# RWKV-7 mixer: the chunk recurrence as one transfer product and one addition a step

## The chip, the core and the metric

The kernel runs on one core of one Trainium2 chip. The metric is the device time of one execution in microseconds. The text uses the profiler's names: PE is TensorE (matmuls), PEld its weight loads, DVE VectorE, ACT ScalarE, POOL GpSimd, SP the queue that issues the transfers. One matmul call on float32 data stands in the trace as two matmul records and two weight-load records; one on float32r data as one of each.

## The reference, cut to what matters

Two decoder layers over 512 positions of width 1024. Each layer is a half feed-forward, a mixer and a half feed-forward. The even layer's mixer is called "ab": an input projection (22 blocks of 128 columns), a Griffin branch, and RWKV-7 time mixing with 8 heads of width 64. This last part is what the change is about:

```python
def step(state, inp):
    r_t, w_t, k_t, v_t, kk_t, a_t = inp
    sa = jnp.einsum('bhvk,bhk->bhv', state, kk_t)
    state = (state * w_t[:, :, None, :]
             - sa[..., None] * (kk_t * a_t)[:, :, None, :]
             + v_t[..., None] * k_t[:, :, None, :])
    return state, jnp.einsum('bhvk,bhk->bhv', state, r_t)
_, y = lax.scan(step, state0, xs)
```

Behind it come a group norm for each head, a bonus term, a gate and the output projection (8 blocks, "ab_out"). The odd layer has another mixer ("c", gated DeltaNet), which the change leaves alone.

## The kernel before

It is one program with an instruction stream for each engine, ordered by hand and joined by semaphores; `wait_ge` makes an engine wait, `then_inc` counts up. Weights stream from HBM through four slots (`RAW`), and ACT and DVE split each into a high and a low float32r part (`WS`), so that each product of the dense blocks is three matmuls (lines 590 to 592). `pe.Fori(1, 4)` is a loop of three passes whose body stands once in PE's stream; a Python `for` writes its body out as many times as it runs.

The 512 positions are cut into 8 chunks (`c`) of 64. A 128-partition tile holds two heads, so there are four blocks `b` of two heads. They are worked in two pairs, `q` = 0 and 1, and in a pair `z` is 0 or 1, so `b = 2q + z`. Every small product is a 64x64 matmul. It reads one half of the partitions (`r`) and writes one half: the same, or for chunks 4 to 7 often the other one (`crossed(r)`). A list in the order `four_ways` goes round all four quarters of the array, `chunk_blocks` and `heads_of` only round the two on the diagonal.

For each pair PE makes the in-chunk products (`triangle_product`, `key_products`, `back_product`), and then inverts a triangular matrix for each head and chunk by doubling. A level is `pe_level_u`, a mask on DVE (line 1989), `pe_level_xx`, a copy on ACT (line 1332), and a transposition on DVE (lines 1979 and 1981). Levels 1 to 3 of both `z` are the `Fori` loop of lines 894 to 902, which also turns one block of keys (`tokens_turned`, `KT` for pair 0, `BT` for pair 1) in each pass. `inside` makes the part of the solution that needs no state: `GT` (the right side for the solve) and `YI` (its outputs). The result of the inversion is `XTF`.

Then comes the recurrence over the chunks (lines 925 to 957), with all 8 heads at once in each product. A step needs, one behind the other: the prediction from the state (L937), an addition on DVE (L2241), the solve with `XTF` (L948), a copy on ACT (L1523), the product with the keys `BT` (L955), and the subtraction on DVE that gives the next state (L2254). The products `KT` with `VT` (L942) and the outputs of the chunk before (`outputs`, L918 and L921) fill gaps. Behind the last chunk DVE adds the outputs (`YF`, L2260), and PE makes the sums for the group norm (L962, L966), the gate (L968) and the output projection.

Of the kernel before, what the change touches and what calls it, by code (L numbers as in the profile page):

```python
# [11 lines left out]
P = 128  # L12
SEQ = 512
# [134 lines left out]
def hybrid_trunk_kernel(nc, x, params, const, w_gate, w_up, w_down, ab_in, ab_out, lru_a, lru_x,  # L148
# [28 lines left out]
    with ExitStack() as ctx:  # L177
# [111 lines left out]
        GT, YI = quad("GT", H_AT + 2 * Q), quad("YI", H_AT + 3 * Q)  # L289
# [24 lines left out]
        SDEC = at("SDEC", SPARE_AT + SEQ + 96, [P, 4, CHUNK])  # L314
# [20 lines left out]
        def ab_mix(t):  # L335
# [22 lines left out]
        predict_mm, predict_added, solve_mm, solve_read, state_mm, state_ready = (sem("predict_mm"), sem("predict_added"), sem("solve_mm"), sem("solve_read"),  # L358
                                                    sem("state_mm"), sem("state_ready"))
# [69 lines left out]
        def head_block(first, rows, e, upper=False):  # L429
# [20 lines left out]
            (predict_mm, 7), (predict_added, 7), (solve_mm, 8), (solve_read, 8), (state_mm, 14), (state_ready, 7),  # L450
# [3 lines left out]
            (exp_ready, 3), (fold_ready, 4), (kk_sq, 4), (ss_max, 4), (bon_in, 4), (bon_mm, 4), (bv_ready, 4), (staged, 6), (level_begun, 34), (fm_ready, 4),  # L454
# [122 lines left out]
        def _(pe):  # L577
# [83 lines left out]
            def tokens_turned(first, src, b, upper, across):  # L661
# [4 lines left out]
                tr.then_inc(tr_mm, 1)  # L666

            def pe_first_u(q, z):
# [4 lines left out]
                if z:  # L673
                    pe.wait_ge(tr_read, 4 * q + 5)
                elif q:
                    pe.wait_ge(xx_read[z], 5)
                else:
                    pe.wait_ge(z_read, AB_BLOCKS)
# [63 lines left out]
            for phase in plan:  # L742
# [19 lines left out]
                if phase == "ab":  # L762
# [85 lines left out]
                    def back_product(q, z):  # L848
# [19 lines left out]

                    for q in range(2):
# [3 lines left out]
                        if q == 0:  # L873
# [3 lines left out]
                            tokens_turned(4, KF, 0, upper=False, across=True)  # L877
                            pe_first_u(q, 0)
                        else:
# [4 lines left out]
                            tokens_turned(4, AL, 0, upper=False, across=False)  # L884
# [9 lines left out]
                        with pe.Fori(1, 4) as l:  # L894
                            pe_level_u(q, 1, l)
                            pe_level_xx(q, 0, l)
                            pe.wait_ge(tr_read, l + 4 * q + 4)
                            pe.wait_ge(staged, l + 3 * q)
                            pe.sem_inc(level_begun, 1)
                            tokens_turned(2, STAGE, 0, upper=False, across=q == 0)  # L900
                            pe_level_u(q, 0, l + 1)
# [9 lines left out]
                    heads_of = [(b, slice(h * CHUNK, (h + 1) * CHUNK)) for b in range(4) for h in range(2)]  # L911

                    def outputs(c, blocks):

                        cc = slice(c * CHUNK, (c + 1) * CHUNK)
                        for b in blocks:
                            for r in (slice(0, CHUNK), slice(CHUNK, P)):
                                mm = pe.matmul(BANK[4 + b][r, cc], GT[r, b, cc], MBT[r, b, cc], start=True, stop=c == 0)  # L918
                            if c:
                                for r in (slice(0, CHUNK), slice(CHUNK, P)):  # L920
                                    mm = pe.matmul(BANK[4 + b][r, cc], SH[r, c, b, :], RF[r, b, cc], start=False, stop=True)  # L921
                            if c == NCHUNK - 1:
                                mm.then_inc(out_mm, 1)

                    for c in range(NCHUNK):
                        cc = slice(c * CHUNK, (c + 1) * CHUNK)
                        if c == 0:
                            for z in range(2):
                                pe.wait_ge(xx_read[z], 10)
                                pe.wait_ge(token_read[z], 4)  # L930
                                pe.wait_ge(mat_ready[z], 8)
                            pe.wait_ge(tr_read, 12)
                            pe.wait_ge(fold_ready, 4)
                        else:
                            pe.wait_ge(state_ready, c)
                            for b, r in heads_of:
                                mm = pe.matmul(BANK[0][r, b * CHUNK:(b + 1) * CHUNK], CPRE[r, b, cc], SH[r, c, b, :], start=True, stop=True)  # L937
# [1660 lines left out]
```

## Time and profile before

| what | us |
|---|---|
| median of 3 runs (2129.04 to 2129.66) | 2129.57 |
| the profiled execution, its own time | 2129.91 |
| span of its trace | 2128.1 |
| of it: inversion of both pairs, 519.4 to 581.2 | 61.8 |
| recurrence over the chunks, 581.2 to 609.6 | 28.4 |
| group norm, gate and first products of the output projection, 609.6 to 636.5 | 26.9 |
| DVE starts the first `YF` | 609.57 |

The profiled execution is 0.34 us above the median. The places in the second part of the table are microseconds from the start of the span. Nearly all of the rest of the span is dense matmuls that follow one another with no gap, so the time of the kernel is the dense products plus what PE loses in the mixers' cores.

### The profile page before, as it was taken

The numbers are of one execution on the slowest core, as the hardware profiler recorded it, in microseconds if no ns is written. First come the engines' busy times: TensorE is split into PE (matmuls) and PEld (weight loads), VectorE is DVE, ScalarE is ACT, GpSimd is POOL, SyncE is SP. The second block draws the span as 40 slices with busy tenths as digits, with TensorE's granted clock in tenths as the row PEclk, the third lists the DMA queues.
The fourth block names the chain that finished last, engine by engine and source line by source line (L and its number), as shares of the span: only waits on it lengthen the run. The fifth ranks groups of instructions, "written<-read, shape, count | busy, mean of one in ns | idle before, by whom it ended". The sixth has DMA issues, their size and how long they took to land. (4 is left out here: it accounts for less than half of the span.)

```text
span 2128.1 us, 33196 instructions
## 1 busy us (share of the span) xinstructions
PE 2077.8 (98%) x13332; PEld 1705.0 (80%) x13332; DVE 1124.0 (53%) x1451; ACT 778.0 (37%) x1175; POOL 165.7 (8%) x120
## 2 busy tenths in 40 slices
PE   7999999999799999999999999999999999999998
PEld 6888888777777888888888888877888878888886
DVE  5444444568757444443444443478776675444422
ACT  4332223383434223322322332245665443323221
POOL 2000011002302000011000001101110120000010
PEclk9999999999999999999999999999999999999999
DMA  4222322320012222332222232221111122222321
GB/s 176 93 99 99 111 95 80 104 70 21 23 61 88 100 96 92 113 100 93 80 99 98 91 118 96 80 81 51 51 51 47 56 80 89 99 99 95 113 95 53
DMA packets 48265, 182.65 MB, mean 86 GB/s; under 512 B 6320, under 2 KB 6576, under 8 KB 48048
## 3 DMA queue, kind: packets, MB, share of 16 engines
q1 hardware_dynamic: 48176, 181.39, 24.8%
q8 instruction: 65, 1.06, 0.2%
q14 instruction: 24, 0.20, 0.0%
HBM read 179.27 MB, written 2.10 MB: 85 GB/s over the span
## 5 line engine op out<-in xcount | busy, mean ns | idle before, releaser
L590 PE MATMUL banks<-H,WS 128*128 128x512 f32 x1840 | 730.8, 397 | 11.4 <-DVE H L1997 8.0
L592 PE MATMUL banks<-H,WS 128*128 128x512 f32 x1840 | 717.6, 390 | 0.0
L591 PE MATMUL banks<-H,WS 128*128 128x512 f32 x1840 | 717.5, 390 | 0.0
L1279 ACT ACTIVATE WS<-RAW 128x1024 fp32r<-128x1024 f32 (+1 forms) x308 | 347.1, 1127 | 931.5 <-PE banks L592 928.1
L1913 DVE TENSOR_TENSOR WS<-RAW,WS 128x1024 fp32r<-128x1024 f32 (+1 forms) x308 | 404.4, 1313 | 231.4 <-ACT WS L1279 231.2
L590 PEld LDWEIGHTS banks<-H,WS 128*128 128x128 f32 x1840 | 346.1, 188 | 91.0 <-DVE WS L1913 11.9
L592 PEld LDWEIGHTS banks<-H,WS 128*128 128x128 f32 x1840 | 346.0, 188 | 72.8
L591 PEld LDWEIGHTS banks<-H,WS 128*128 128x128 f32 x1840 | 346.3, 188 | 71.4 <-issue 2.4
L590 PE MATMUL banks<-A,WS 128*128 128x512 f32 x704 | 273.9, 389 | 0.0
L591 PE MATMUL banks<-A,WS 128*128 128x512 f32 x704 | 273.9, 389 | 0.0
L592 PE MATMUL banks<-A,WS 128*128 128x512 f32 x704 | 273.9, 389 | 0.0
L1780 POOL TENSOR_TENSOR ACC<-ACC,US 128x512 f32<-128x512 f32 x49 | 92.8, 1894 | 1364.2 <-issue 1006.3
L1953 DVE TENSOR_TENSOR US<-banks,RSTD 128x512 f32<-128x512 f32 x88 | 60.8, 691 | 248.8 <-PE banks L592 248.8
L1953 DVE TENSOR_TENSOR GS<-banks,RSTD 128x512 f32<-128x512 f32 x88 | 60.8, 691 | 180.1 <-PE banks L592 180.1
L590 PEld LDWEIGHTS banks<-A,WS 128*128 128x128 f32 x704 | 132.1, 188 | 27.7
L592 PEld LDWEIGHTS banks<-A,WS 128*128 128x128 f32 x704 | 132.1, 188 | 27.3
L591 PEld LDWEIGHTS banks<-A,WS 128*128 128x128 f32 x704 | 132.1, 188 | 27.3
L1925 DVE SCALAR_TENSOR_TENSOR X<-banks,X 128x512 f32 (+1 forms) x48 | 33.1, 690 | 158.8 <-PE banks L592 158.8
L1316 ACT ACTIVATE A<-US 128x512 f32 (+1 forms) x88 | 55.7, 633 | 47.5 <-DVE US L1960 47.2
L1960 DVE TENSOR_TENSOR US<-GS,US 128x512 f32<-128x512 f32 x88 | 60.9, 693 | 9.1
L1965 DVE TENSOR_TENSOR A<-US,A 128x512 f32 (+1 forms) x88 | 60.3, 685 | 2.8 <-ACT A L1316 2.8
L1311 ACT ACTIVATE GS<-GS 128x512 f32<-128x512 f32 x88 | 54.1, 615 | 13.6 <-DVE GS L1953 13.6
(388 smaller groups left out, 1660.5 us busy)
## 6 DMA issues: line engine op xcount, KB each, us to landing
RAW<-in_w_gate SPq DMA_DIRECT2D x88, 512.0 KB, 3.2
RAW<-in_w_up SPq DMA_DIRECT2D x88, 512.0 KB, 3.2
RAW<-in_w_down SPq DMA_DIRECT2D x64, 704.0 KB, 4.0
RAW<-in_c_in SPq DMA_DIRECT2D x32, 512.0 KB, 3.2
RAW<-in_ab_in SPq DMA_DIRECT2D x22, 512.0 KB, 3.2
RAW<-in_ab_out SPq DMA_DIRECT2D x8, 512.0 KB, 5.6
RAW<-in_c_out SPq DMA_DIRECT2D x8, 512.0 KB, 3.2
X<-in_x SPq DMA_DIRECT2D x4, 512.0 KB, 7.1
```

What stands on the lines that cost most here:

```text
L590: pe.matmul(bank[:, :], high[:, cols], upper, start=first and j == 0, stop=False)
L591: pe.matmul(bank[:, :], high[:, cols], lower, start=False, stop=False)
L592: mm = pe.matmul(bank[:, :], low[:, cols], upper, start=False, stop=last and j == len(rows) - 1)
L1279: act.activation(WS[:, 0, c % SPLIT, 0:cols] if dst is None else dst, RAW[:, c % RING, 0:cols], ACT.Copy).then_inc(hi_ready, 1)
L1311: act.activation(GS[:, j, :], GS[:, j, :], ACT.Silu).then_inc(silu_ready[j], 1)
L1316: act.activation(A[:, 0, 2 * i + j, :], US[:, j, :], ACT.Copy).then_inc(ahi_ready[j], 1)
L1780: pool.tensor_tensor(ACC[:, :], ACC[:, :], US[:, j, :], ALU.add).then_inc(acc_ready[j], 1)
L1913: vec.tensor_tensor(WS[:, 1, c % SPLIT, 0:cols], RAW[:, c % RING, 0:cols], WS[:, 0, c % SPLIT, 0:cols].bitcast(F32), ALU.subtract).then_in ...
L1925: vec.scalar_tensor_tensor(X[:, 2 * i + j, :], bank[:, :], factor, X[:, 2 * i + j, :], ALU.mult, ALU.add).then_inc(x_ready[j], 1)
L1953: vec.tensor_tensor((GS, US)[k][:, j, :], (GATE, UP)[k][j][:, :], RSTD[:, :], ALU.mult).then_inc((gs_ready, us_ready)[k][j], 1)
L1960: vec.tensor_tensor(US[:, j, :], GS[:, j, :], US[:, j, :], ALU.mult).then_inc(prod_ready[j], 1)
L1965: vec.tensor_tensor(A[:, 1, 2 * i + j, :], US[:, j, :], A[:, 0, 2 * i + j, :].bitcast(F32), ALU.subtract).then_inc(act_ready[j], 1)
```

## The change

The step of the recurrence is linear in the state, so a whole chunk can be written as one 64x64 matrix for each head (the transfer, `MT`) and one addition (`NS`): state(c+1) = MT(c)' state(c) + NS(c). Both are made ahead of the recurrence, for all chunks of a block.

- The prediction keys `CPRE`, weighted by the decay of the chunk before (`prior_fold` on POOL, into `PRIOR_STAGE`), are turned on PE into `PT`, one block in pair 0's prologue and one in each pass of its loop, and copied by ACT (`prior_copied`).
- `inner(b)` applies `XTF` to `GT` and to `PT` at once: 32 matmul calls a block, one behind the other on the same quarter. ACT (for blocks 2 and 3 half of it DVE) copies both with the sign turned: the new `GT`, and `WT`.
- `transfer(b)` (12 calls) gives `MT` = `WT` with `BT` plus a diagonal of decays (`DIAG`, made on POOL; added on POOL for blocks 0 and 1, on DVE for 2 and 3). `additions(b)` (28 calls) gives `NS` = `KT` with `VT` plus `BT` with `GT`.
- `corrections(b)` (14 calls) and an addition on DVE fold the in-chunk correction into the queries `RF`. `within(b)` (16 calls) makes the outputs that need no state, and `carried(c)` (8 calls) adds those from the state.
- A step is then `state_step(c)` (8 calls) and `state_added(c)` on DVE, for c = 1 to 6. The old loop over the chunks goes.
- Pair 1's loop of levels is written out, with `inner`, `transfer` and `additions` of blocks 0 and 1 between its levels. Pair 0's loop stays a loop, its body longer by one `tokens_turned`.
- `back_product` and the turning of `AL` go round four quarters where they went round two. `YI`, `MT`, `DIAG`, `PT` and `NS` take places of tiles that are done with. Ahead of the levels PE also waits for the `inside` copies of the second block (`token_read[1]`).

```diff
-GT, YI = quad("GT", H_AT + 2 * Q), quad("YI", H_AT + 3 * Q)
+GW = at("GW", H_AT + 2 * Q, [P, 2, 4, SEQ])
+GT, WT = GW[:, 0], GW[:, 1]
+NS, MT = quad("NS", H_AT), quad("MT", ACT_AT + 4 * Q)
+YI, DIAG = quad("YI", ACT_AT + 8 * Q), quad("DIAG", ACT_AT + 9 * Q)
+PT, PRIOR_STAGE = quad("PT", WS_AT), at("PRIOR_STAGE", WS_AT + Q, [P, 1, SEQ])
...
                 pe.wait_ge(mat_ready[z], 4 * q + 3)
-                for r, c in chunk_blocks():
+                for r, a, c in four_ways:
                     cc = slice(c * CHUNK, (c + 1) * CHUNK)
-                    mm = pe.matmul(BANK[4 * z + 2][r, cc], AL[r, b, cc], RF[r, b, cc], start=True, stop=True)
+                    mm = pe.matmul(head_block(4 * z + 2, a, c), AL[r, b, cc], RF[r, b, cc], start=True, stop=True)
                 mm.then_inc(mat_mm[z], 1)
...
+            def inner(b):
+                q, z = divmod(b, 2)
+                pe.wait_ge(xx_read[z], 5 * q + 5)
+                pe.wait_ge(token_read[z], 2 * q + 2)
+                if b == 0:
+                    pe.wait_ge(prior_read, 4)
+                    pe.wait_ge(token_read[1], 4)
+                if b == 1:
+                    pe.wait_ge(m_copied, 1)
+                for r, a, c in four_ways:
+                    cc = slice(c * CHUNK, (c + 1) * CHUNK)
+                    pe.matmul(head_block((6, 6, 0, 4)[b], a, c), XTF[r, b, cc], GT[r, b, cc], start=True, stop=True)
+                    mm = pe.matmul(head_block((6, 6, 0, 4)[b], a, c, upper=True), XTF[r, b, cc], PT[r, b, cc], start=True, stop=True)
+                mm.then_inc(inner_mm, 1)
...
+            def transfer(b):
+                inner_done(b)
+                pe.wait_ge(tr_read, 9 + b)
+                if b >= 2:
+                    pe.wait_ge(n_read, b - 1)
+                for r, a, c in four_ways:
+                    if 0 < c < NCHUNK - 1:
+                        cc = slice(c * CHUNK, (c + 1) * CHUNK)
+                        mm = pe.matmul(head_block((6, 6, 6, 2)[b], r, c), WT[a, b, cc], BT[a, b, cc], start=True, stop=True)
+                mm.then_inc(m_mm, 1)
+            def additions(b):
+                inner_done(b)
+                if b == 0:
+                    pe.wait_ge(m_copied, 2)
+                if b == 1:
+                    pe.wait_ge(tr_read, 12)
+                for r, a, c in four_ways:
+                    if c < NCHUNK - 1:
+                        cc = slice(c * CHUNK, (c + 1) * CHUNK)
+                        to = head_block((6, 2, 0, 4)[b], r, c)
+                        pe.matmul(to, KT[a, b, cc], VT[a, b, cc], start=True, stop=False)
+                        mm = pe.matmul(to, BT[a, b, cc], GT[a, b, cc], start=False, stop=True)
+                mm.then_inc(n_mm, 1)
+            def corrections(b):
+                if b % 2 == 0:
+                    pe.wait_ge(m_vec, b // 2 + 1)
+                for r, a, c in four_ways:
+                    if c:
+                        cc = slice(c * CHUNK, (c + 1) * CHUNK)
+                        mm = pe.matmul(head_block((6, 6, 2, 2)[b], r, c, upper=b % 2), WT[a, b, cc], MBT[a, b, cc], start=True, stop=True)
+                mm.then_inc(corr_mm, 1)
+            def out_block(b, r, c):
+                return head_block(4 + b // 2 * 2, r, c, upper=b % 2)
...
+            def within(b):
+                if b == 0:
+                    pe.wait_ge(n_read, 4)
+                if b == 2:
+                    pe.wait_ge(rf_ready, 2)
+                for r, a, c in four_ways:
+                    cc = slice(c * CHUNK, (c + 1) * CHUNK)
+                    mm = pe.matmul(out_block(b, r, c), GT[a, b, cc], MBT[a, b, cc], start=b % 2 == 0 and c % TT == 0, stop=False)
+                mm.then_inc(within_mm, 1)
...
+            def state(c, b, r):
+                return SH[r, c, b, :] if c > 1 else NS[r, b, 0:CHUNK]
+            def state_step(c):
+                cc = slice(c * CHUNK, (c + 1) * CHUNK)
+                if c > 1:
+                    pe.wait_ge(state_ready, c - 1)
+                for b, r in heads_of:
+                    mm = pe.matmul(BANK[0][r, b * CHUNK:(b + 1) * CHUNK], MT[r, b, cc], state(c, b, r), start=True, stop=True)
+                mm.then_inc(state_mm, 1)
+            def carried(c):
+                cc = slice(c * CHUNK, (c + 1) * CHUNK)
+                for b, r in heads_of:
+                    mm = pe.matmul(out_block(b, r, c), state(c, b, r), RF[r, b, cc], start=False, stop=b % 2 == 1 and c % TT == TT - 1)
+                    if c == NCHUNK - 1 and r.start:
+                        mm.then_inc(out_mm, 1)
+            def level_pair(q, l, then=None):
+                pe_level_u(q, 1, l)
+                pe_level_xx(q, 0, l)
+                pe.wait_ge(tr_read, l + 4 * q + 4)
+                pe.wait_ge(staged, l + 3 * q)
+                if q == 0:
+                    pe.sem_inc(level_begun, 1)
+                tokens_turned(2, STAGE, 0, upper=False, across=True)
+                if then is not None:
+                    transfer(then)
+                pe_level_u(q, 0, l + 1)
+                pe_level_xx(q, 1, l)
             for q in range(2):
                 if q == 0:
                     triangle_product(0, 0)
                     key_products(q, 1)
                     pe.wait_ge(bv_ready, 2)
                     tokens_turned(4, KF, 0, upper=False, across=True)
+                    pe.wait_ge(prior_staged, 1)
+                    pe.wait_ge(tr_mm, 5)
+                    tokens_turned(4, PRIOR_STAGE, 0, upper=True, across=False, done=prior_mm)
                     pe_first_u(q, 0)
                 else:
                     pe_first_u(q, 0)
                     key_products(q, 0)
                     key_products(q, 1)
                     pe.wait_ge(xx_read[1], 5)
-                    tokens_turned(4, AL, 0, upper=False, across=False)
+                    tokens_turned(4, AL, 0, upper=False, across=True)
...
-                    pe_level_xx(q, 1, l)
+                pe.wait_ge(token_read[1], 2 * q + 2)
                 if q == 0:
+                    with pe.Fori(1, 4) as l:
+                        level_pair(0, l)
+                        pe.wait_ge(prior_staged, l + 1)
+                        pe.wait_ge(prior_read, l)
+                        pe.sem_inc(level_begun, 1)
+                        tokens_turned(6, PRIOR_STAGE, 0, upper=False, across=False, done=prior_mm)
                     triangle_product(1, 0)
+                else:
+                    level_pair(1, 1)
+                    inner(0)
+                    level_pair(1, 2, then=0)
+                    inner(1)
+                    level_pair(1, 3, then=1)
+                    pe.sem_inc(level_begun, 3)
+                    additions(0)
                 pe_level_u(q, 1, 4)
                 pe_last_xx(q, 0)
                 if q == 0:
                     triangle_product(1, 1)
+                else:
+                    additions(1)
                 pe_last_xx(q, 1)
...
+            inner(2)
+            inner(3)
+            transfer(2)
+            transfer(3)
+            additions(2)
+            additions(3)
+            corrections(0)
+            corrections(1)
+            pe.wait_ge(n_read, 4)
+            pe.wait_ge(m_pool, 2)
+            pe.wait_ge(m_vec, 2)
+            state_step(1)
+            corrections(2)
+            corrections(3)
+            state_step(2)
+            within(0)
+            within(1)
+            state_step(3)
+            within(2)
+            within(3)
+            state_step(4)
+            pe.wait_ge(rf_ready, 4)
+            pe.wait_ge(within_mm, 4)
+            carried(1)
+            carried(2)
+            state_step(5)
+            carried(3)
+            carried(4)
+            state_step(6)
+            carried(5)
+            carried(6)
+            pe.wait_ge(state_ready, 6)
+            carried(7)
...
@@ ScalarE @@
+    def inner_copied(b, k):
+        act.wait_ge(inner_mm, b + 1)
+        act.activation(GW[:, :, b, k * HALF_BANK:(k + 1) * HALF_BANK], PS[:, (6, 6, 0, 4)[b] + k, :].rearrange("p (u c) -> p u c", u=2),
+                       ACT.Copy, scale=-1.0).then_inc(inner_act, 1)
...
+        if q == 0:
+            branch_hi(l - 1)
+        elif l > 1:
+            transfer_copied(l - 2)
         level_copied(q, 1, l)
+        if q == 0:
+            prior_copied(l)
+        elif l < 3:
+            inner_copied(l - 1, 0)
+            inner_copied(l - 1, 1)
+        else:
+            additions_copied(0)
...
@@ GpSimd @@
-    fold(0, CPRE, 2)
     stage(0, 2)
+    prior_fold(2)
     branch_lo(0)
+    stage(0, 3)
     branch_lo(1)
+    prior_fold(3)
...
     stage(1, 1)
-    fold(0, RF, 3)
-    fold(1, CPRE, 2)
+    query_fold(0)
+    branch_lo(2)
+    branch_lo(3)
+    diagonals()
+    query_fold(1)
     stage(1, 2)
-    fold(1, RF, 3)
     stage(1, 3)
+    for b in range(2):
+        transfer_kept(b)
...
@@ VectorE @@
+    def state_added(c):
+        vec.wait_ge(state_mm, c)
+        vec.tensor_tensor(SH[:, c + 1, :, :], BANK[0][:, 0:4 * CHUNK].rearrange("p (b v) -> p b v", v=CHUNK),
+                          NS[:, :, c * CHUNK:(c + 1) * CHUNK], ALU.add).then_inc(state_ready, 1)
+    inner_kept(2)
+    inner_kept(3)
+    transfer_kept(2)
+    transfer_kept(3)
+    queries_corrected(0)
+    state_added(1)
+    queries_corrected(1)
+    state_added(2)
+    queries_corrected(2)
+    state_added(3)
+    queries_corrected(3)
+    for c in range(4, NCHUNK - 1):
+        state_added(c)
```

## Rows read from the trace of the kernel before

**Rows 1.** The page: the span, and PE's busy time, share and instructions.
```profile
span 2128.1 us, 33196 instructions
PE 2077.8 (98%) x13332; PEld 1705.0 (80%) x13332; DVE 1124.0 (53%) x1451; ACT 778.0 (37%) x1175; POOL 165.7 (8%) x120
```

**Rows 2.** Windows: length, busy us (instructions) of each engine, PE's clock, DMA share, GB/s.
```profile
581.20:609.60 28.40, 23.28 (x690) 20.64 (x692) 10.89 (x28) 4.96 (x10) 0.00 (x0) 1.00 0.22 78
609.60:636.50 26.90, 26.71 (x116) 18.15 (x113) 20.55 (x28) 13.57 (x17) 0.53 (x1) 1.00 0.23 79
519.40:581.20 61.80, 48.76 (x2178) 45.85 (x2177) 46.85 (x89) 23.34 (x41) 30.16 (x26) 1.00 0.01 3
```

**Rows 3.** Timeline of one step of the recurrence: start, length, engine, instruction, [idle before <-releaser].
```profile
587.81 0.68 PE L937 MATMUL banks<-SH,FACTORS 64*64 64x64 f32 x16 [0.59 <-DVE SH L2254]
...
588.61 0.42 DVE L2241 TENSOR_TENSOR GT<-GT,banks 128x256 f32<-128x256 f32 x1 [0.85 <-PE banks L937]
...
589.93 0.38 ACT L1523 ACTIVATE GT<-banks 128x256 f32<-128x256 f32 x1 [3.45 <-PE banks L948]
...
590.37 0.68 PE L955 MATMUL banks<-GT,KBT 64*64 64x64 f32 x16
591.17 0.42 DVE L2254 TENSOR_TENSOR SH<-SDEC,banks 128x256 f32<-128x256 f32 x1 [1.36 <-PE banks L955]
...
591.65 0.68 PE L937 MATMUL banks<-SH,FACTORS 64*64 64x64 f32 x16 [0.59 <-DVE SH L2254]
```

**Rows 4.** Timeline of half a pass of pair 0's level loop.
```profile
541.18 0.69 PE L697 MATMUL banks<-XX,TM 64*64 64x64 f32 x32 [0.33 <-ACT XX L1332]
...
541.66 0.68 PE L707 MATMUL banks<-IU,XT 64*64 64x64 f32 x32
...
542.40 0.60 ACT L1332 ACTIVATE XX<-banks 128x512 f32<-128x512 f32 x1 [0.87 <-PE banks L707]
542.49 0.69 DVE L1989 TENSOR_TENSOR IU<-banks,CST 128x512 f32<-128x512 f32 x1
...
543.10 0.43 DVE L1979 STREAM_TRANSPOSE XT<-XX 128x256 f32<-128x256 f32 x1
543.14 0.69 PE L697 MATMUL banks<-XX,TM 64*64 64x64 f32 x32 [0.80 <-ACT XX L1332]
```

**Rows 5.** Timeline of PE: where it idles for no releaser ("issue"), and pair 1's levels.
```profile
535.92 0.50 PE L707 MATMUL banks<-IU,XT 64*64 64x64 f32 x18 [0.78 <-issue]
...
550.56 0.91 PE L716 MATMUL banks<-XT,IU 64*64 64x64 f32 x24 [0.34 <-issue]
...
554.75 0.92 PE L664 MATMUL banks<-CST,AL 64*64 64x64 f32 x25 [0.37 <-issue]
...
561.92 0.62 PE L866 MATMUL banks<-MKM,VT 64*64 64x64 f32 x26 [0.43 <-issue]
...
564.00 0.69 PE L697 MATMUL banks<-XX,TM 64*64 64x64 f32 x32 [0.53 <-ACT YI L1339]
...
565.70 0.63 PE L707 MATMUL banks<-IU,XT 64*64 64x64 f32 x27 [0.90 <-issue]
```

**Rows 6.** Windows from one such stall to the next, and inside pair 0's loop.
```profile
550.56:554.75 4.19, 3.82 (x127) 3.69 (x128) 2.01 (x4) 0.60 (x1) 4.11 (x4) 1.00 0.03 6
554.75:561.92 7.17, 6.74 (x256) 6.60 (x256) 6.27 (x12) 1.79 (x3) 2.13 (x2) 1.00 0.02 5
561.92:565.70 3.78, 2.35 (x125) 2.14 (x125) 1.85 (x4) 2.07 (x4) 0.00 (x0) 1.00 0.02 4
538.90:548.00 9.10, 7.14 (x400) 6.70 (x402) 8.87 (x19) 5.62 (x11) 5.77 (x6) 1.00 0.00 0
```

**Rows 7.** DMA queue of instructions: packets, MB, share; whole span, then 549 to 566.
```profile
q8 instruction: 65, 1.06, 0.2%
...
q8 instruction: 4, 0.07, 1.7%
```

**Rows 8.** Timeline: DVE's first additions behind the recurrence.
```profile
609.57 2.48 DVE L2260 TENSOR_TENSOR YF<-banks,YI 128x512 f32<-128x512 f32 x4 [1.72 <-PE banks L921]
```

More of the change, by code:

```diff
@@ new lines, in _ @@
+                    heads_of = [(b, slice(h * CHUNK, (h + 1) * CHUNK)) for b in range(4) for h in range(2)]
+                    def state(c, b, r):
[7 more added lines that the diff above has]
+                        mm.then_inc(state_mm, 1)
@@ L908, in _ @@
                             triangle_product(1, 1)
+                        else:
+                            additions(1)
                         pe_last_xx(q, 1)
[L911 to L923, printed above, removed]
@@ L957, in _ @@
-                    outputs(NCHUNK - 1, range(4))
+                    inner(2)
[11 more added lines that the diff above has]
+                    corrections(2)
@@ L1520, in _ @@
                         act_inverse(q)
-                    for c in range(NCHUNK):
-                        act.wait_ge(solve_mm, c + 1)
-                        act.activation(GT[:, :, c * CHUNK:(c + 1) * CHUNK], BANK[2][:, 0:4 * CHUNK].rearrange("p (b v) -> p b v", v=CHUNK),
-                                       ACT.Copy).then_inc(solve_read, 1)
-                        if c in (5, 6):
-                            split_hi(u0 + AB_BLOCKS + c - 5, 0)
-                    act.wait_ge(out_mm, 4)
+                    inner_copied(2, 0)
+                    inner_copied(3, 0)
+                    additions_copied(2)
+                    additions_copied(3)
+                    for m in range(2):
+                        split_hi(u0 + AB_BLOCKS + m, 0)
+                    act.wait_ge(within_mm, 4)
                     for m in (2, 3):
@@ L1821, in branch_lo, with before_chunk, query_fold @@
                 pool.tensor_tensor(YA_LO[:, b, :], GG[:, b, :], YA_HI[:, b, :].bitcast(F32), ALU.subtract).then_inc(ya_lo, 1)
-            def fold(q, t, written):
+            def before_chunk(q, blocks):
+                return PEND[:, q:q + blocks, 0:NCHUNK - 1].unsqueeze(3).to_broadcast([P, blocks, NCHUNK - 1, CHUNK])
+            def query_fold(q):
                 for z in range(2):
-                    pool.wait_ge(mat_mm[z], 3 * q + written)
-                part = t[:, 2 * q:2 * q + 2, CHUNK:SEQ].rearrange("p b (c k) -> p b c k", k=CHUNK)
-                pend = PEND[:, 2 * q:2 * q + 2, 0:NCHUNK - 1].unsqueeze(3).to_broadcast([P, 2, NCHUNK - 1, CHUNK])
-                pool.tensor_tensor(part, part, pend, ALU.mult).then_inc(fold_ready, 1)
+                    pool.wait_ge(mat_mm[z], 3 * q + 3)
+                part = RF[:, 2 * q:2 * q + 2, CHUNK:SEQ].rearrange("p b (c k) -> p b c k", k=CHUNK)
+                pool.tensor_tensor(part, part, before_chunk(2 * q, 2), ALU.mult).then_inc(fold_ready, 1)
@@ new lines, in diagonals @@
+            def diagonals():
+                pool.wait_ge(bv_ready, 4)
+                pool.wait_ge(tr_mm, 4)
+                blocks = DIAG[:, :, :].rearrange("p b (c k) -> p b c k", k=CHUNK)
+                for b in range(4):
+                    pool.memset(blocks[:, b, 0, :], 0.0)
+                    ins = pool.tensor_tensor(blocks[:, b, 1:NCHUNK, :], half("ident")[:, 1:NCHUNK, :],
+                                             PEND[:, b, 0:NCHUNK - 1].unsqueeze(2).to_broadcast([P, NCHUNK - 1, CHUNK]), ALU.mult)
+                    if b % 2:
+                        ins.then_inc(diag_ready, 1)
@@ L1831, in stage, with transfer_kept @@
+            def transfer_kept(b):
+                pool.wait_ge(m_copied, b + 1)
+                pool.wait_ge(diag_ready, 1)
+                pool.tensor_tensor(MT[:, b, :], MT[:, b, :], DIAG[:, b, :], ALU.add).then_inc(m_pool, 1)
             def stage(q, l):
@@ new lines, in inner_kept, with transfer_kept @@
+                    def inner_kept(b):
+                        vec.wait_ge(inner_mm, b + 1)
+                        vec.tensor_scalar(GW[:, :, b, HALF_BANK:SEQ], PS[:, (0, 4)[b - 2] + 1, :].rearrange("p (u c) -> p u c", u=2), -1.0, None,
+                                          ALU.mult).then_inc(inner_vec, 1)
+                    def transfer_kept(b):
+                        vec.wait_ge(m_mm, b + 1)
+                        vec.wait_ge(diag_ready, 2)
+                        vec.tensor_tensor(row_by_head(MT[:, b, :]), two_banks((6, 2)[b - 2]), row_by_head(DIAG[:, b, :]),
+                                          ALU.add).then_inc(m_vec, 1)
```

140 lines of the change are left out of this document (58 added, 82 removed).

## Prediction

> **What bounds the kernel now.** I read the page first: PE is busy for 98% of the span [rows 1], so a change in this mixer can only win or lose what PE spends there. The windows by stage come next [rows 2]. From 519.4 to 581.2 (the inversion of both pairs) DVE works 46.9 of 61.8 us. In the recurrence nothing is full: PE 23.3 of 28.4 us, DVE 10.9, ACT 5.0; it is a chain of latencies. Behind it PE is busy 26.7 of 26.9 us, so what the first `YF` gains or loses on 609.57 [rows 8] goes straight into the kernel's time. The clock is 1.00 of full speed in all three, and plays no part.
>
> The timeline of one step [rows 3] shows the chain: L937, 0.68 us; DVE, 0.42; L948; ACT, 0.38; L955, 0.68; DVE, 0.42; the next L937 starts 3.84 us behind the last. Seven such steps make the stage.
>
> In a pass of the level loop [rows 4] two chains are about full. DVE goes mask 0.69, transpositions, mask, with no idle. PE's L697 waits for ACT's copy, which waits for L707. Behind L707 PE has a gap (0.80 us idle before 543.14, about 1.0 counted from its last issue).
>
> The fourth reading decides. Five times PE idles with no releaser, "issue" [rows 5]. The three windows between the last four of these [rows 6] hold 127, 256 and 125 matmul records: one, two and one times 128, within the 2% of records that can be missing. In 549 to 566 the instruction queue moved 4 packets, of 16.3 KB each by the page (1.06 MB in 65) [rows 7]. So PE's stream comes in pieces that hold 128 matmul records with their weight loads, and PE had to wait for pieces: 15.14 us for four, 3.79 each; the last three took 3.65, the first 4.19. The next piece is evidently asked for only when the one before it is entered. Inside the loop (538.9 to 548.0) 400 records ran in 9.1 us and the DMA moved nothing [rows 6]: what a loop repeats is not fetched again. So straight-line code gets at most 128 records in about 3.7 us, 35 a microsecond, whatever the array could do: L707 puts 32 through in 0.68 us [rows 4]. The old recurrence is below the limit, 690 in 28.4 us [rows 2], 24 a microsecond.
>
> **The change part by part.** I take the engines' work first, then the supply.
>
> *The chain.* A step keeps one product (0.68), a hand-over (0.12, from 588.49 to 588.61), one addition (0.42) and one back (0.06, from 591.59 to 591.65): 1.28 instead of 3.84 us. Six steps are left. `queries_corrected` and `within` sit between them (DVE 0.69 each by the nearest row, the mask [rows 4]) and make three steps about 1.45. With the last three `carried` I get 9.0 us from the first `state_step` to the first `YF`.
>
> *Ahead of it.* From the end of pair 1's inversion: `inner` of blocks 2 and 3, their copies (ACT and DVE, 0.6 each), two `transfer`, two `additions`, two `corrections`, one copy. 172 calls. Round four quarters a call takes 0.03 us (32 records in 0.48), round two 0.06 (L716: 24 records in 0.91 with a tail of 0.22). `inner` and `additions` stay on one quarter for two calls, which no row shows; I take 0.04, between the two: 120 calls at 0.04, 52 at 0.03, and a last copy with its hand-overs, 0.8. That makes 7.2 us, bounds 6 (all at 0.03) and 10 (0.06).
>
> *Between the levels of pair 1.* Two `inner` (1.3 us each) go into gaps of 1.0, `additions` into one of 1.0 and one of 0.5: 1.2 us more. The wait for both `inside` copies costs about 0.1, as `back_product` is shorter. In pair 0 the turning of 16 blocks round two quarters (0.93) fits its gap of 1.0 but not behind the last pass, where `triangle_product`, DVE's mask and POOL's next triangle are queued: 0.7. POOL's new folds and `DIAG` (some 8 us) fit, as POOL works only 30 of 61.8 us [rows 2]; were they late, pair 1's turnings would be. ACT's added copies fall into its waits for L707 (0.87 idle at 542.40 [rows 4]).
>
> Sum of this: old, 581.2 to 609.57 is 28.4. New is 7.2 + 9.0 + 1.2 + 0.1 + 0.7 = 18.2, less 0.9, since `inner(2)` starts at the end of the last L716 (580.3) and not behind its copy (581.2). So the engines' work alone would give about 11 us, between 7 and 14.
>
> *The supply.* Pair 1's loop is now written out and everything behind it is straight-line. Count records from the levels of pair 1 on (32 for a call list of 16): three passes 480, `inner` 128, `transfer` 48, `additions` 112, last level 96; then 344 up to the first `state_step` (128 + 48 + 112 + 56); then 392 (steps 96, `corrections` 56, `within` 128, `carried` 112). That is 1600, and some 25 for semaphore instructions. Before, it was 704 with a loop that fetched nothing.
>
> Where the borders fall: before, one lay 45 records into pair 0's loop (32 + 13 before 535.92 [rows 5]). The new turning ahead of the loop shifts this to 13. The body has 192 records, so a second border falls into its first pass, at record 141, in the last L707. Entered at 535.2, the next piece is there at about 539.1, where the work would be at 537.8: 1.3 us late, once. From there, with 0.7 from above: the third border lies 70 records behind the loop's end, reached at 549.3. The fourth is reached at 554.3 and the fifth at 558.2, set by work (DVE and POOL, 2.0 behind the old times). The sixth is 561.7 and the seventh 565.4, set by supply. There 26 records are left ahead of the levels. 26 + 1625 = 1651 records are 12 pieces and 115 records: 12 x 3.7 = 44.4 gives 609.8, and the last piece holds two steps and five `carried`, 3.4 us to the first `YF`. So `YF` starts at 613.2, against 609.57: **3.65 us later**. The tail is PE's and keeps its length.
>
> 3.7 is my choice: the mean of four is 3.79, that of the last three 3.65. Each 0.1 us is worth 1.2: with 3.5 `YF` is 2.4 us earlier, with 3.79 1.1 later, with 4.19 5.9 later. The borders up to 565.4 are uncertain by 1 to 2 us more.
>
> Edits costed at nothing: `back_product` and `AL` round four quarters save 0.45 us each, but the supply takes it back; the early `MORE_HI` splits on ACT are not waited for. The first output weights are asked for at the end of the inversion, now some 12 us later, 10 us ahead of their split, so they are in time. If they were late, the output projection would wait.
>
> The Trainium skill speaks for the change here. Its page "Runtime: NRT & Kernel Launch", section "Instruction fetch mechanics", says that fetching is hidden because dispatch is slower than the refill, and that full unrolling is to be preferred. By that rule the supply would cost nothing, and the sum would be the first rival's below. The rows with "issue" disagree for these small products: 0.34 to 0.90 us idle at each border [rows 5].
>
> **The rivals.**
>
> *The supply does not bind* (the other side). Pieces might be asked for further ahead in a stream without loops. Against it: four stalls, each 128 or 256 records behind the last. For it: the stretch from 519.5 to 535.92 shows one such stall only. Then 2129.57 - 11 = 2118.6. It decides where a piece comes in less than 3.0 us (3.7 less 8 / 12): from there the kernel is faster by over 4.3 us.
>
> *The supply binds at half strength.* Where PE waits for semaphores its sequencer may ask early, and a piece then costs about 3.2 us. Twelve pieces save 6, so the kernel is 2 us faster than before, 2127.2; down to 2124.
>
> *Pair 0's loop is fetched again.* Its body now touches three pieces, with a fourth loaded ahead. The trace shows three kept (two and one ahead), not four. If the fourth drives out the first, each of two passes takes three pieces' time, 11.1 in place of 3.9 us: 14 us more, 2148.
>
> **How the numbers follow.** The sum against the profiled execution's own time is 2129.91 + 3.65 = 2133.6. That execution is 0.34 above the median, so on the median it is 2133.2; I say 2133.3. Chances: supply binds as summed 0.77 (2129 to 2139 by the interval's 3.5 to 4.0 and the borders), half strength 0.09, not at all 0.08, loop fetched again 0.06. 0.2% is 4.3 us, about what a measurement of this kernel can tell from no change. My forecast lies just inside it, so the first case splits into 0.37 slower, 0.39 same, 0.01 faster; half strength 0.02 faster, 0.07 same. In all: faster 0.11, same 0.46, slower 0.43. The range 2125 to 2139.5 takes in the first case and most of the second.
>
> **What would show it.** Right: "issue" waits of up to 2 us in every stretch of about 128 matmul records from 560 on, instruction packets every 3.5 to 4 us up to the first `YF`, PE idle where the state chain is ready, steps about 1.4 us apart but broken by such waits, `YF` at 613. Wrong: packets closer than 3 us, or windows with 50 records a microsecond in straight-line code; `inner` waiting for ACT; packets inside pair 0's loop; a chain of waits in which DVE or ACT ends what PE waits for.

## The result, and the profile after

The changed kernel takes 2139.45 us (median of 5 runs, 2138.76 to 2139.8), the kernel before 2129.37: a ratio of 1.0046, interval 1.0036 to 1.0057. It is 10.1 us slower. The forecast was 2133.3, 3.7 above the 2129.57 that it was made from, with a range up to 2139.5. The sign and the mechanism were right, the size was not: the time lies inside the range by 0.05 us, and that much is luck. The 2129 to 2139 that the prediction gave the case in which the supply binds as summed do not hold it.

The page of the changed kernel's profile, to be held against [rows 1], shows 448 more matmuls and 1.1 us more of PE's busy time for a span 9.2 us longer. What was added is waiting. (The profiled execution took 2139.09 us, 9.2 more than that of before; the argument below goes by these two.)

```profile
span 2137.3 us, 34085 instructions
...
PE 2078.9 (97%) x13780; PEld 1707.8 (80%) x13780; DVE 1121.9 (52%) x1438; ACT 785.0 (37%) x1183; POOL 173.0 (8%) x133
```

DVE's timeline has the first `YF` at 618.57 instead of 609.57 [rows 8]. The rest of the span keeps its length: 1518.7 behind it, 1518.5 before.

```profile
618.57 2.48 DVE L2469 TENSOR_TENSOR YF<-banks,YI 128x512 f32<-128x512 f32 x4 [0.74 <-PE banks L971]
```

So the 9 us lie ahead of 618.57. PE's timeline there, where it idles with no releaser (the stalls of [rows 5]), goes on to the end, one in every piece of the stream (these are six of them):

```profile
565.69 0.68 PE L875 MATMUL banks<-MKM,VT 64*64 64x64 f32 x29 [0.82 <-issue]
567.60 1.13 PE L705 MATMUL banks<-XX,TM 64*64 64x64 f32 x32 [1.23 <-issue]
...
574.56 0.21 PE L891 MATMUL banks<-PT,XTF 64*64 64x64 f32 x1 [1.43 <-issue]
...
578.63 0.62 PE L705 MATMUL banks<-XX,TM 64*64 64x64 f32 x26 [1.65 <-issue]
...
597.43 0.29 PE L890 MATMUL banks<-GW,XTF 64*64 64x64 f32 x3 [1.07 <-issue]
...
604.24 0.27 PE L924 MATMUL banks<-GW,KBT 64*64 64x64 f32 x1 [3.69 <-issue]
```

Windows cut at every 256th instruction of PE (128 matmuls, 128 weight loads), with the columns of [rows 2]; the last covers them all:

```profile
565.35:570.63 5.28, 3.71 (x126) 3.40 (x125) 1.05 (x2) 1.81 (x4) 0.75 (x2) 0.69 0.01 3
...
570.63:574.22 3.59, 2.25 (x127) 2.08 (x127) 2.99 (x7) 1.06 (x2) 0.51 (x1) 0.98 0.02 5
574.22:578.29 4.07, 2.42 (x126) 2.09 (x125) 2.02 (x4) 2.66 (x5) 1.34 (x2) 1.00 0.01 4
...
597.10:603.90 6.80, 2.63 (x125) 2.39 (x125) 1.98 (x3) 1.20 (x2) 0.00 (x0) 1.00 0.73 270
...
603.90:607.61 3.71, 3.37 (x127) 3.38 (x128) 0.61 (x1) 2.12 (x3) 0.00 (x0) 0.64 0.02 7
...
611.34:614.95 3.61, 3.01 (x128) 2.87 (x127) 1.45 (x3) 1.60 (x2) 0.00 (x0) 1.00 0.02 5
...
565.35:618.57 53.22, 35.57 (x1629) 33.43 (x1628) 20.44 (x40) 18.08 (x29) 4.40 (x5) 0.94 0.13 44
```

The reader is to see that each piece takes 3.5 to 4.1 us while PE works 2.2 to 3.4 us in it, and that no engine is full. Two pieces are longer, 5.28 and 6.80. The twelve from 565.35 to 614.95 take 49.6 us; the forecast had 12 x 3.7 = 44.4. Without the two, ten take 37.5, 3.75 each. All twelve together average 4.13, above the 3.5 to 4.0 that the prediction allowed a piece.

**The longest piece.** The DMA view of 595.8 to 601.6 has no line for the instruction queue; its 16 engines are 85.5% busy with the output weights, which SP issued at 595.00. One packet had begun at 595.17, ahead of this window, and the next begins at 602.05, behind it: 6.9 us later, where the others from 568.64 on are 3.5 to 4.0 us apart. (An expectation below has this start at 601.71; nothing hangs on the difference.)

```profile
595.00 2.44 SPq L527 DMA_DIRECT2D RAW<-in_ab_out  x4
...
GB/s 0 198 28 85 141 282 311 424 395 395 395 367 311 170 28 141 113 113 198 198 339 367 367 311 282 424 396 339 367 424 424 396 367 367 339 367 396 424 396 424
...
q1 hardware_dynamic: 461, 1.71, 85.5%
issues: line engine op xcount, KB each, median us to landing
RAW<-in_ab_out SPq DMA_DIRECT2D x3, 512.0 KB, 6.8
```

**The piece of 5.28.** PE enters it at 565.35 and issues `inside`. Then it stands at the wait that the change added, for `inside`'s copy of the second block: ACT ends that copy at 567.50, and L705 starts at 567.60. The next instruction packet starts at 568.64, 3.3 us into the piece, where in the pieces entered without such a wait it starts 1.4 to 1.9 us in.

```profile
566.91 0.59 ACT L1477 ACTIVATE YI<-banks 128x512 f32<-128x512 f32 x1
```

The granted clock was low in this piece too, 0.69. But in the run with one call for two products (below), which has the same wait, the piece is as long at a clock of 1.00, so it is not the clock that makes it:

```profile
564.26:569.56 5.30, 2.55 (x126) 2.19 (x125) 2.08 (x5) 2.17 (x4) 1.53 (x2) 1.00 0.01 3
```

### The profile page after: what moved, and what is told of

It reads as the page before. It is cut to its first block and busy times, and to the rows that moved or that the text cites. A ratio compares the mean times of both kernels' runs of the same rounds, so it can differ in the third digit from the quotient of the medians.

```text
span 2137.3 us, 34085 instructions
## 1 busy us (share of the span) xinstructions
PE 2078.9 (97%) x13780; PEld 1707.8 (80%) x13780; DVE 1121.9 (52%) x1438; ACT 785.0 (37%) x1183; POOL 173.0 (8%) x133
```

## The experiments

Theory 1: PE runs at the speed at which its instructions arrive, 128 matmul records in 3.7 us of straight code, longer where a packet is asked for late or queues behind weights. Theory 2: copies of ACT and DVE between dependent products set the end. Theory 3: the array time of the added matmuls does. Where a second time stands beside a result, it is that of the kernel before, run beside it; differences to the changed kernel are to its 2139.45 (2138.76 to 2139.8). A ratio is to the kernel before, with its 95% interval. "Piece" is the prediction's word for 128 matmul records with their weight loads, which come in one instruction packet.

### The levels of pair 1 in a loop again

```diff
-level_pair(1, 1); inner(0); level_pair(1, 2, then=0); inner(1); level_pair(1, 3, then=1); additions(0)
+with pe.Fori(1, 4) as l:
+    level_pair(1, l)
...
+# inner(0), transfer(0) between the last products; the rest of blocks 0, 1 behind them
```

> The changed kernel with pair 1's levels 1 to 3 back in a loop of three passes, as before the change; the inner values and transfers of blocks 0 and 1 and the additions stand behind the levels instead of between them. The computation is the whole one. Theory 1 (PE works at the speed at which its instructions arrive, about 3.7 us for 128 matmul records, and a loop's later passes need none that are new): two of the three passes, at about 240 records each, arrive no more; they take about 4 us each instead of 7, and the kernel is 3 to 6 us faster than the changed one, 2133 to 2137 us. Theory 2 (copies of ACT and DVE between dependent products set the end): the chain of inner values, transfers and additions begins later, so no gain or up to 4 us slower, 2139 to 2143 us. Theory 3 (array time of the added matmuls): the same matmuls, so no change, 2139 us.

Measured: 2137.11 us (1.0035, 1.0022 to 1.0049), 2.3 less; the first `YF` at 616.53, 2.0 earlier. The sign is theory 1's (theory 2 had it slower), the size just short of its range, and the intervals of the two kernels overlap, so this run alone settles little. The windows say where the gain went: the loop's stretch had 503 records in 12.68 us, 3.2 us for 128 (at a mean granted clock of 0.87), but the same output weights, now asked for at 586.63, lengthened another piece to 7.04.

```profile
571.05:583.73 12.68, 9.99 (x503) 9.46 (x503) 10.55 (x21) 4.93 (x9) 1.23 (x2) 0.87 0.01 3
590.66:597.70 7.04, 2.77 (x137) 2.63 (x132) 0.69 (x1) 1.43 (x3) 1.27 (x1) 0.91 0.42 151
```

### One piece more

```diff
 for r, a, c in four_ways:
+    if b < 2:
+        one = slice(c * CHUNK, c * CHUNK + 1)
+        pe.matmul(head_block(6, a, c)[:, 0:1], XTF[r, b, cc], GT[r, b, one], start=True, stop=True)
+        pe.matmul(head_block(6, a, c, upper=True)[:, 0:1], XTF[r, b, cc], PT[r, b, one], start=True, stop=True)
```

> The changed kernel with 64 more matmul calls of one output column each in the inner values of blocks 0 and 1; their results are overwritten by the calls behind them, so the outputs are those of the reference. They are 128 more matmul records of one column. Theory 1 (instruction arrival): one piece of 128 records more, +3.7 us (3 to 4.5), about 2143 us. Theory 2 (copies between dependent products) : they lie in idle time of PE between copies, 0 to +1 us. Theory 3 (array time by columns): 128 records of one column instead of 64 are at most a few tenths of a microsecond in the array, +0 to +1 us.

Measured: 2146.53 us (1.0080, 1.0066 to 1.0093), 7.1 more. Theories 2 and 3 had at most 1 us and fall as they were put, but 7.1 is also well above one piece. In the profiled execution the first `YF` is 7.2 us later, at 625.74. Of this, 2.0 lie ahead of the added matmuls: the stall of L875 ends at 567.70 instead of 565.69. A low clock at 540 to 544, alone among the profiled executions here, made PE's pass 1.2 us later there (545.25 instead of 544.09). The other 5.2 are one piece, 3.7, and 1.5 more, for which the windows show the clock:

```profile
540.00:544.00 4.00, 4.00 (x145) 3.97 (x134) 2.02 (x4) 1.64 (x3) 2.14 (x2) 0.57 0.02 4
...
573.48:578.00 4.52, 4.52 (x129) 4.52 (x127) 2.02 (x4) 0.60 (x1) 0.00 (x0) 0.61 0.02 4
578.00:583.29 5.29, 5.29 (x134) 5.29 (x135) 0.43 (x1) 1.09 (x2) 0.00 (x0) 0.50 0.02 3
583.29:586.56 3.27, 3.08 (x139) 2.99 (x132) 2.27 (x5) 2.29 (x4) 1.41 (x2) 0.79 0.02 5
```

The granted clock is 0.50 through the second of these pieces, the lower level of 1.2 GHz, and 0.61 on the mean of the first, and PE is busy all the time. The two take 2.3 us more than two of 3.75, the third 0.5 less. This account was made behind the result: no run took the clock's share by itself, so this experiment shows that added records cost more than theories 2 and 3 allow, and not how much one piece costs.

### Only the loop written out, in the kernel before

```diff
-with pe.Fori(1, 4) as l:
-    level_pass(l)
+for l in range(1, 4):      # pair 1 only
+    level_pass(l)
```

> The kernel before the change with one edit: pair 1's levels 1 to 3 are written out as three passes instead of a loop, in the same order with the same waits. Same computation and same instructions executed but for the loop's own. Theory 1 (instruction arrival): some 256 records of passes two and three have to arrive anew, at 3.7 us for 128 instead of the passes' 3.96 us each: the recurrence behind has slack only where PE waits for copies, so +2 us (1 to 4), about 2131.5 us. Theories 2 and 3: nothing executed differs, so 0, 2129.4 us.

Measured: 2133.74 us against 2129.59 (1.0019, 1.0010 to 1.0028), 4.2 more. PE does the same work in the same order, so the way in which instructions reach it costs this by itself, and the clock is 1.00 throughout this stretch. The size was forecast too small. The same 768 instructions of PE (windows of the kernel before, then of this one; up to 3% of the matmul records are missing) take 8.63 and 13.40 us, and the instruction queue moves no packet in the first and three in the second:

```profile
567.24:575.87 8.63, 7.03 (x375) 6.82 (x378) 8.39 (x18) 4.18 (x7) 2.87 (x3) 1.00 0.00 0
```

```profile
566.57:579.97 13.40, 7.86 (x387) 7.17 (x381) 9.71 (x21) 4.22 (x8) 2.34 (x3) 1.00 0.02 4
...
q8 instruction: 3, 0.05, 1.7%
```

That is 4.5 us a piece and not 3.7: the waits for copies and the waits for pieces do not overlap well, which I put down to packets asked for late, as below. It is not shown.

### The same extra matmuls where the supply has room

```diff
 mm.then_inc(state_mm, 1)   # kernel before, last product of a step
+for b, r in heads_of:
+    pe.matmul(BANK[0][r, (4 + b) * CHUNK:(4 + b) * CHUNK + 1], BT[r, b, cc], GT[r, b, c * CHUNK:c * CHUNK + 1], start=True, stop=True)
```

> The kernel before the change with 56 more matmul calls of one output column, eight behind the last product of each of the recurrence's first seven steps, into a part of a bank that nobody reads, so the outputs are the reference's. They are 112 more matmul records, 16 in each step. Theory 1 (instruction arrival binds only where PE has more than about 128 records in 3.7 us): the step of before has 96 records in 3.7 to 3.8 us, with 16 more it stays under the bound, so 0 to +1 us, 2129.5 to 2130.5 us, against +7.1 us for 128 records in the changed kernel. Theory 3 (such a record has a price of its own wherever it stands, 7.1 us for 128): +6 us, 2135.6 us.

Measured: 2129.21 us against 2129.44 (1.0001, 0.9991 to 1.0010): nothing. The steps still start 3.7 to 3.8 us apart, with 0.18 us of idle time where [rows 3] have 0.59. 112 records cost nothing here. They took up 0.41 us of PE's idle time in each step, so this run shows only that they are free where PE has time to spare. But PE had such time in the changed kernel too, 1.0 to 1.7 us with no releaser in most of its pieces, and there 128 records cost 5.2 us of the profiled execution (about 3 with all taken off that the low clock may have cost). A price of the record itself, as theory 3 has it, would have been hidden there as it is here.

```profile
590.83 0.68 PE L937 MATMUL banks<-SH,FACTORS 64*64 64x64 f32 x16 [0.18 <-DVE SH L2256]
594.68 0.51 PE L937 MATMUL banks<-SH,FACTORS 64*64 64x64 f32 x10 [0.18 <-DVE SH L2256]
```

### One piece less

```diff
-pe.matmul(head_block(first, a, c), XTF[r, b, cc], GT[r, b, cc], start=True, stop=True)
-mm = pe.matmul(head_block(first, a, c, upper=True), XTF[r, b, cc], PT[r, b, cc], start=True, stop=True)
+mm = pe.matmul(both_blocks(first, a, c), XTF[r, b, cc], GT_and_PT[r, :, b, cc], start=True, stop=True)
```

> The changed kernel with the two products of a head and chunk in the inner values (inner values and prediction keys, same stationary operand) as one call with a moving operand of 2 x 64 columns. Same computation, same columns through the array; 64 calls of two passes fewer, which is 128 matmul records fewer, one piece. Theory 1 (instruction arrival): one piece of 3.7 us less, 3.7 us faster than the changed kernel (2.5 to 5), about 2135.7 us. Theory 2 (copies between dependent products): nothing of the copies changes, 0, 2139.4 us. Theory 3 (array time): the same columns, 0 to 1 us faster.

Measured: 2135.44 us (1.0027, 1.0017 to 1.0037), 4.0 less; the slowest of its nine executions, 2137.39, is below the fastest of the changed kernel. The columns through the array are the same; only the count of instructions is down. From the stall in `inside` (L875 in the changed kernel, L876 here) to the first `YF` 1501 records stand in place of 1629, and the instruction queue moves one packet less, as theory 1 had it; theories 2 and 3 had at most 1 us. That the gain comes out at the size of one piece is in part chance. In the profiled execution the first `YF` is 3.0 us earlier. Of this, 1.1 lie ahead of that stall, before any edited product, and behind it a gain of 3.7 meets a packet that the output weights held up longer, with a pause of 5.07 us where the changed kernel had 3.69. (`GT_and_PT` stands for one view of memory that holds both tiles.)

```profile
564.75:615.57 50.82, 34.70 (x1501) 32.45 (x1496) 20.31 (x39) 18.05 (x29) 4.18 (x5) 0.93 0.13 45
...
600.96 0.36 PE L925 MATMUL banks<-GP,KBT 64*64 64x64 f32 x1 [5.07 <-issue]
```

### The two late pieces, one at a time and together

```diff
-pe.wait_ge(token_read[1], 2 * q + 2)
+if q == 0: pe.wait_ge(token_read[1], 2)
```

> The changed kernel without the wait for the second block's inside copy ahead of pair 1's levels (inner values of block 0 have that wait themselves, so no product needs it there). Same computation. Theory 1 (a piece's successor is asked for some way into the piece, so that a wait early in a piece delays the next one: the border of 570.63 us was 5.3 us behind the one before it instead of 3.7): 1.6 us faster than the changed kernel (0.8 to 2), about 2137.8 us. Theory 2 (copies): the levels' own copies are as late as before, 0 to 0.5 us faster.

```diff
+# SP, ahead of output weights 2, 3 and 4
+sp.wait_ge(n_mm, 4) / sp.wait_ge(state_mm, 3) / sp.wait_ge(state_mm, 5)
```

> The changed kernel with the second to fourth of the output weights' four transfers of 512 KB held back on SP until later products of PE have begun, so that PE's instruction packets do not queue behind all four at once. Same computation. Theory 1 (the fetch that began at 601.71 instead of about 598.4 us stood behind these transfers): the pause of PE of 3.9 us ending at 603.90 shrinks to about 1 us, and the kernel is 2 to 3.3 us faster, 2136 to 2137.5 us. Theories 2 and 3: nothing of the transfers bears on copies or array time before they are used, 0, 2139 us; if the weights then come late for the output products, slower.

> The changed kernel with two edits at once: no wait for the second block's inside copy ahead of pair 1's levels, and the output weights' transfers held back on SP. Same computation, all instructions of the changed kernel but one wait, three waits more on SP. Theory 1 (the forecast's pieces of 3.7 us, with two of them late, one behind a wait and one behind weight transfers): both late pieces go, and the time comes down to about the forecast of the prediction: the two measured gains of 2.7 and 2.4 us add, 2134.3 us (2133 to 2136). If the late pieces are not what separates forecast and result, or if one delay only takes the place of the other, no more than the larger of the two: 2136.7 us.

Measured: without the wait 2136.71 us (2.7 less; first `YF` at 616.19), with the transfers spaced 2137.04 (2.4 less, but only 0.9 in the profiled span: its late piece shrank from 6.80 to 4.61, while its other pieces took 3.9), both 2134.40 (5.0 less, 1.0021, 1.0012 to 1.0030). The intervals of the first two (1.0022 to 1.0046 and 1.0023 to 1.0050) reach into that of the changed kernel, though each of their executions is faster than its fastest; that of both edits does not. Windows, without the wait, with the transfers spaced, and with both:

```profile
565.63:569.42 3.79, 2.33 (x141) 2.14 (x135) 2.02 (x4) 2.06 (x4) 0.61 (x1) 1.00 0.02 4
595.31:602.13 6.82, 2.64 (x141) 2.39 (x135) 1.98 (x3) 1.19 (x2) 0.00 (x0) 1.00 0.62 232
```

```profile
598.60:603.21 4.61, 2.64 (x141) 2.39 (x138) 1.98 (x3) 1.19 (x2) 0.00 (x0) 1.00 0.03 9
```

```profile
566.01:610.81 44.80, 30.98 (x1524) 29.00 (x1515) 19.56 (x37) 15.96 (x27) 3.79 (x5) 0.96 0.12 39
...
613.77 2.48 DVE L2471 TENSOR_TENSOR YF<-banks,YI 128x512 f32<-128x512 f32 x4 [0.74 <-PE banks L973]
```

The piece of 5.28 us becomes 3.79, the other stays until the transfers are spaced, and is 4.50 then with both edits. The twelve pieces take 44.80 us, 3.73 each, and `YF` starts at 613.77: the forecast's sum was 44.4 and 613.2. The effects add (2.7 + 2.4 = 5.1). Profiled executions differ by 1.1 us, in the second experiment by 2.0, ahead of the first edited place. Counted from the stall in `inside` there (L875 in the changed kernel) to the first `YF`, it is 52.9 us in the changed kernel, 50.8 without the wait, 52.6 with the transfers spaced and 48.1 with both. So spacing alone is not well resolved; its share is better read from 2136.71 to 2134.40.

### All at once, and a version that beats both

Loop, one call for two products, no wait, spaced transfers:

> The changed kernel with four edits at once: pair 1's levels in a loop with the inner values, transfers and additions behind it; the two products of the inner values as one call; no wait for the second block's inside copy ahead of the levels; the output weights' transfers held back on SP. Same computation. Theory 1 (instruction arrival): the loop gave 2.3 us and the transfers 2.4 us, one piece less gives 3.7 us and the wait 1.6 us; together 8 to 10 us faster than the changed kernel, 2129.5 to 2131.5 us, which is about the kernel before. Theory 2 (copies): no more than the 2.3 and 2.4 us that are measured, 2134.7 us or above.

Measured: 2129.68 us against 2129.44 (0.9998, 0.9989 to 1.0007), 9.8 less than the changed kernel, as theory 1 had it, and 5 below the least that theory 2 allowed. The single gains (2.3, 2.4, 4.0 and 2.7) would add to 11.4, so they overlap a little. On top of it, for blocks 2 and 3, the transfer product and the query correction, which share `WT`:

```diff
-mm = pe.matmul(head_block(first, r, c), WT[a, b, cc], BT[a, b, cc], start=True, stop=True)
+mm = pe.matmul(both_blocks(first, r, c), WT[a, b, cc], BT_and_MBT[a, :, b, cc], start=True, stop=True)
...
-corrections(2)
-corrections(3)
```

> The kernel with the four edits at once, and one more: transfer product and query correction of the third and fourth block (same stationary operand) as one call with 2 x 64 columns. Same computation; 24 calls of two passes fewer, 48 matmul records, which is 0.38 of a piece. Theory 1 (instruction arrival): 1.4 us less than with the four edits, 2128.3 us (2127.5 to 2129), just below the kernel before. Theory 2 (copies) and theory 3 (array time): 0, 2129.7 us.

Measured: 2126.92 us against 2129.42 (0.9987, 0.9978 to 0.9996), faster than the kernel before by 2.5 us and than the changed one by 12.5. It was 2.8 less than with four edits where 1.4 were expected; the intervals of the two reach into each other. `YF` starts at 606.39.

```profile
606.39 2.48 DVE L2478 TENSOR_TENSOR YF<-banks,YI 128x512 f32<-128x512 f32 x4 [0.74 <-PE banks L980]
```

## Why the prediction was right in its mechanism and short in its size

- *What bounds the kernel.* Right, in the profiled executions: the tail kept its length, and 9.0 of the 9.2 us of span are in `YF`'s start.
- *The supply.* Right, and shown: writing out a loop costs 4.2 us with nothing else changed, and one piece fewer gives 4.0, part of which is chance, where the other theories have at most 1.
- *Records and borders.* Right: the seventh border was forecast at 565.4 and is at 565.35; from there 1651 records were forecast, and 1629 stand in the trace. The last piece took 3.62 (forecast 3.4). Pair 0's loop was late once, by 1.2 us (forecast 1.3), and not fetched again: in 541 to 550 no instruction packet moved.
- *The term that failed is "12 x 3.7 = 44.4".* It is 49.6 in the changed kernel: ten pieces at 3.75, one of 5.28 and one of 6.80. 565.35 + 49.60 + 3.62 = 618.57. Behind the first stands the new wait, which the prediction priced at 0.1 us by what it holds up on the engine and not by what it does to the next packet. It cost 1.5 us of the piece, and taking it away gave 2.7. Behind the second stands the sentence that the output weights are "in time". The tail kept its length, so they were, but while they come PE's packet waits too. Spacing them gave 2.3 to 2.4. Together they bring the kernel to 2134.4, 1.1 from the forecast. The prediction's own 3.7 for a piece that nothing holds up was right.
- *The sum of the engines alone* (11 us gained, 7 to 14) was never reached and is not shown. The version of 2126.92 still follows the supply: from 585 to 604 its instruction packets start 3.4 to 3.9 us apart.
- *The clock "plays no part"*: true of this stretch in the kernel before, and carried over to the changed kernel without a reason. There it stood at 0.50, the lower level of 1.2 GHz, from 567.4 to 570.7 and from 605.0 to 608.3. It cost little: the piece from 603.90 took 3.71 us with 3.37 busy, and that from 565.35 is as long at 1.00. With more records, in the second experiment, two pieces at 0.61 and 0.50 took 2.3 us more than two of 3.75.
- *The range* held the time by 0.05 us, which is luck: the error of the sum is 6.2 us.
- *The rivals.* Supply not binding and half strength are excluded by the stalls at every border, with ten pieces at 3.75 us; the loop fetched again did not happen.
- *The Trainium skill.* By the Trainium skill ("Runtime: NRT & Kernel Launch", section "Instruction fetch mechanics") fetching is hidden and full unrolling preferred. Here the loop written out is slower by 4.2 us, so for 64x64 float32 products the measurement decides against it.

What stays open: that a packet is asked for some way into a piece, and that a wait early in it delays it, is read from the starts of packets. It fits all profiled executions: with the wait, that packet starts 5.3 to 5.6 us behind the one before it (five kernels), without it 3.6 to 4.2 (four). But the moment of asking was not measured by itself. What took the clock down was not tried either: in this stretch PE had stood in such pauses before each fall, but others as long left it at 1.00, as in the kernel before with its loop written out.

## What to carry to other kernels

Where a stage is made of many small matmuls, count the instructions as well as the latencies: here the stream gives 128 float32 matmul records in about 3.7 us, so a shorter dependency chain bought with more calls in straight-line code can lose. Calls that share the stationary operand, taken as one with a wider moving operand, and loops kept as loops are worth more there than saved latency. In such a stage place large transfers and waits with the fetches in mind: the two late packets here were worth 5.0 us together.

## What the runs showed that I had not expected

Weight transfers of 2 MB held up an instruction packet by about 3 us (6.80 us for a piece, 4.50 to 4.61 with the transfers spaced). One wait early in a piece, with PE's array idle for 1.2 us at it, cost 2.7 us. And the clock, at 1.00 through this whole stretch of the kernel before, stood at 0.50 to 0.69 in single pieces of some of the kernels whose PE paused for instructions; one such piece, of cheap matmuls, was busy for all of its 5.29 us.
